# Fourier branch over even and odd parts, scans by halves of the groups, compressed scores of both heads at once, in a two-block float32 model

## The reference

```python
s = jnp.einsum('bgrcd,bgnd->bgrcn', qc, kc) * ATTN_SCALE          # compressed scores, 31 keys
p_cmp = masked_softmax(s, cmp_end[None, :] <= tpos[:, None])
o_cmp = jnp.einsum('bgrcn,bgnd->bgrcd', p_cmp, vc)

def _fourier_mix(u):                                              # u: 512 tokens x 512 channels
    ug = u.reshape(b, l, FOURIER_GROUPS, FOURIER_GROUP_CH)        # 4 groups of 128 channels
    f = jnp.fft.fft2(ug, axes=(1, 3), norm='ortho').real
    return f.reshape(b, l, FOURIER_WIDTH)

def _ssm_direction(ug, ..., reverse):                             # 32 groups, 64 complex states
    bu = jnp.einsum('blgc,gnc->blgn', ug, b_bar)
    _, h = lax.associative_scan(_scan_combine, (a, bu), axis=1, reverse=reverse)
    return jnp.einsum('blgn,gcn->blgc', h, c_mat).real            # forward and backward are added

merged = gates[..., :D_MODEL] * (y_f @ w_fourier_out) + gates[..., D_MODEL:] * (y_s @ w_ssm_out)
x = x + merged @ w_out
x = x + _hier_moe(hn, ...)                                        # 64 experts, 1024 -> 512 -> 1024
```

## Time and profile before

| | us |
|---|---|
| time, median of 3 runs | 2460.68 |
| lowest and highest of them | 2452.25, 2461.19 |
| the profiled execution | 2447.28 |
| its span, first to last instruction | 2445.4 |
| TensorE busy | 2226.5 (91%) |
| VectorE busy | 612.2 (25%) |
| ScalarE busy | 323.1 (13%) |
| GpSimd busy | 206.8 (8%) |
| mean granted TensorE clock | 0.971 of full |

### The profile page before, as it was taken

The page is one execution under the profiler, slowest core; times in us unless marked ns, Lnnn a source line. Parts: engine busy times, 40 slices in busy tenths (PEclk is TensorE's granted clock), DMA queues, the critical chain, the costliest instruction groups (busy, mean ns, idle before and its releaser), DMA issues.

```text
span 2445.4 us, 20383 instructions
## 1 busy us (share of the span) xinstructions
PE 2226.5 (91%) x8284; PEld 1022.6 (42%) x8284; DVE 612.2 (25%) x1311; ACT 323.1 (13%) x652; POOL 206.8 (8%) x186
## 2 busy tenths in 40 slices
PE   8999999999999999999999999988888888877886
PEld 4554444445444444466644463333323333322332
DVE  2246544311633210033431142111111111111114
ACT  2014424202111100021110120000000000000001
POOL 0001111010344200000000001000000000000001
PEclk9999999999999999998999999998999999999998
DMA  6201010322232321219422339999999999999995
GB/s 273 86 35 69 35 69 4 151 103 78 95 118 79 141 77 72 101 52 161 155 102 83 159 156 408 426 426 426 425 426 426 426 427 427 425 425 422 421 426 221
DMA packets 69759, 552.43 MB, mean 226 GB/s; under 512 B 21656, under 2 KB 26392, under 8 KB 37600
## 3 DMA queue, kind: packets, MB, share of 16 engines
q1 hardware_dynamic: 42384, 515.49, 51.8%
q10 hardware_dynamic: 17200, 23.23, 3.2%
q0 software_dynamic: 10080, 12.38, 1.4%
HBM read 543.91 MB, written 35.68 MB: 237 GB/s over the span
## 4 chain that ended last, share of the span: by engine, by line
PE 69%; DMA 26%; DVE 3%; ACT 1%; issue 1%; DVEq 0%; POOL 0%; SPq 0%; ACTq 0%; POOLq 0%
PE ps L380 25%; DMA sb<-in_eu 12%; PE ps L1008 9%; PE ps L456 8%; DMA sb<-in_eg 8%; PE ps L698 8%; PE ps L1040 4%; DMA sb<-in_ed 4%; PE ps L399 2%; PE ps L856 2%; PE ps L628 2%; PE ps L541 1%; PE ps L574 1%; PE ps L568 1%; DMA sb<-in_mgg 1%
## 5 line engine op out<-in xcount | busy, mean ns | idle before, releaser
L380 PE MATMUL ps<-sb 128*128 128x512 f32 (+2 forms) x1536 | 613.8, 559 | 2.8 <-issue 1.4
L1008 PE MATMUL ps<-sb 128*64 128x512 f32 x2048 | 487.7, 632 | 108.6 <-DMA sb<-in_eu 79.3
L380 PEld LDWEIGHTS ps<-sb 128*128 128x128 f32 x1536 | 279.7, 190 | 315.9 <-issue 312.6
L1008 PEld LDWEIGHTS ps<-sb 128*64 128x64 f32 x2048 | 176.7, 145 | 398.8 <-issue 398.7
L1040 PE MATMUL ps<-sb 128*64 128x512 f32 x992 | 232.5, 623 | 26.9 <-ACT sb L1427 17.2
L456 PE MATMUL ps<-sb 128*128 128x512 f32 x512 | 236.1, 600 | 0.3 <-DMA sb<-in_mgg 0.3
L698 PE MATMUL ps<-sb 128*128 128x512 f32 x448 | 192.5, 592 | 0.7 <-ACT sb L1247 0.7
L1451 DVE TENSOR_TENSOR sb<-sb 128x32 f32<-128x32 f32 (+10 forms) x292 | 115.4, 412 | 115.7 <-PE ps L662 66.2
L1040 PEld LDWEIGHTS ps<-sb 128*64 128x64 f32 x992 | 73.7, 143 | 164.2 <-issue 137.6
L456 PEld LDWEIGHTS ps<-sb 128*128 128x128 f32 x512 | 91.3, 190 | 100.0 <-issue 98.9
L698 PEld LDWEIGHTS ps<-sb 128*128 128x128 f32 x448 | 85.0, 190 | 107.6 <-issue 107.6
(11 more groups left out here) (283 smaller groups left out, 1481.5 us busy)
## 6 DMA issues: line engine op xcount, KB each, us to landing
sb<-in_eg SPq DMA_DIRECT2D x64, 2048.0 KB, 33.6
sb<-in_eu SPq DMA_DIRECT2D x63, 2048.0 KB, 33.9
sb<-in_ed SPq DMA_DIRECT2D x63, 2048.0 KB, 32.4
sb<-in_m SPq DMA_DIRECT2D x16, 2048.0 KB, 7.4
sb<-in_mg SPq DMA_DIRECT2D x8, 1536.0 KB, 6.9
sb<-in_winF SPq DMA_DIRECT2D x5, 2048.0 KB, 7.3
sb<-in_mgg SPq DMA_DIRECT2D x4, 2048.0 KB, 8.0
sb<-in_wo SPq DMA_DIRECT2D x4, 2048.0 KB, 7.3
```

What stands on the lines that cost most here:

```text
L380: ins = pe.matmul(out, lhsT, rhs, start=k == 0, stop=k == len(pieces) - 1)
L1008: ins = pe.matmul(o[64 * e:64 * e + 64, :], x[:, k, 64 * e:64 * e + 64], weight(2 * mat + e)[:, 512 * k:512 * k + 512], start=k == 0, stop ...
```

## The change

Three things are changed.

1. **Fourier branch.** The transform over 512 tokens is folded. GpSimd makes the sum and the difference of token t and token 512-t (`EO[0]` and `EO[1]`, two instructions of 4x255 values a partition, the second operand read backwards, and two small ones for token 0). The channel transform is then cosine on the sums and sine on the differences, over 256 tokens: 16 products of 128 columns in 4 tiles, and 4 products of 128 columns with a single row for token 256 (`v256`), which ScalarE writes into row 0 of the odd part. The token transform takes 4 products of 512 columns for each channel group where it took 8. The table `dft` is half as large. TensorE waits for the semaphore `eo` where it waited for the copies of `ufT`. The products `within` stand in pairs before `yf` 2 and `yf` 3.
2. **Scans.** VectorE does the state space work in two halves of 16 groups. The first half starts after six of the eight backward copies and the `v` tiles of its groups; the last two copies come after its first six instructions. `borders(0)` still waits for `sp` at 4, which is now the first half; `borders(2)` waits for 8. The expert loads' first wait is `sp` at 8. GpSimd clears the border columns of `Sp` by halves, behind its new work.
3. **Compressed scores.** A turn covers both head halves of a token block: 8 products of 31 columns, three recurrent steps, 8 transposes, one more step. VectorE's steps after the mask addition cover 8x31 values and are 4 turns in place of 8.

```diff
-                for h in range(2):
-                    dve.wait_ge(*T.full("cs", i, h))
-                    if n > 3:
-                        dve.wait_ge(*T.full("ct", (n - 4) // 2, h))
+                    after(own(dve.tensor_reduce(st, s3, op=ALU.max, axis=AX.X)))
+                    dve.tensor_tensor(s3, s3, bc(st, 2, 31), ALU.subtract).then_inc(S("csub"), 1)
+                    yield 2
+                    dve.wait_ge(S("cexp"), i + 1)
...
+                    dve.tensor_tensor(s3, s3, bc(st, 2, 31), ALU.mult).then_inc(S("cprob"), 1)
+                    yield 1
+                    copy(("ct", i, 1), PCT[32:63, :, 128 * i:128 * i + 128],
+                         T.ap("ct", i, 1)[0:31, :].rearrange("p (a b) -> p a b", a=4))
+                    yield 1
```

```diff
-            for i in range(4):
-                for gp in range(2):
-                    o = open_tile(pe, ("vf", i, gp), any_bank())
-                    for q in range(2):
-                        ins = pe.matmul(o[:, 256 * q:256 * q + 256], ufT[:, 2 * gp + q, 128 * i:128 * i + 128], ck("cs"), start=True, stop=True)
-                    ins.then_inc(T.f("vf", i, gp), 1)
+            pe.wait_ge(S("eo"), 4)
+            for b in range(2):
+                for part in range(2):
+                    o = open_tile(pe, ("vf", b, part), any_bank())
+                    for g in range(4):
+                        ins = pe.matmul(o[:, 128 * g:128 * g + 128], EO[part][:, g, 128 * b:128 * b + 128],
+                                        ck("cs")[:, 128 * part:128 * part + 128], start=True, stop=True)
+                    ins.then_inc(T.f("vf", b, part), 1)
...
-                chain(o, [(Vf[:, k % 4, g, 128 * (k // 4):128 * (k // 4) + 128], cf[:, k // 4, k % 4, :]) for k in range(8)], ("yf", g))
+                chain(o, [(Vf[part][b][:, g, :], cf[:, part, b, :]) for b in range(2) for part in range(2)], ("yf", g))
...
             gate_tile(0, 0, 0)
+            pe.wait_ge(S("sp"), 8)
             borders(2)
```

```diff
-            pool.wait_ge(S("sp_in"), 1)
-            pool.memset(Sp[0:64, :, :, 0], 0.0).then_inc(S("sp_zero"), 1)
-            pool.memset(Sp[64:128, :, :, 63], 0.0).then_inc(S("sp_zero"), 1)
+            for m in range(4, 8):
+                pool.wait_ge(*T.free("z2", m))
+            pool.wait_ge(S("m2w"), 7)
+            for n, op in enumerate((ALU.add, ALU.subtract)):
+                pool.tensor_tensor(EO[n][:, :, 1:256], ufT[:, :, 1:256], ufT[:, :, 511:256:-1], op).then_inc(S("eo"), 1)
+            pool.tensor_copy(EO[0][:, :, 0:1], ufT[:, :, 0:1]).then_inc(S("eo"), 1)
+            pool.memset(EO[1][:, :, 0:1], 0.0).then_inc(S("eo"), 1)
```

More of the change, by code:

```diff
@@ L288, in program @@
         Sp = view(zone, 16384, 2, 32, 64)
-        Vf = view(WR[2], 0, 4, 4, 256)
+        EO = [view(WR[2], 1024 * n, 4, 256) for n in range(2)]
+        Vf = [[view(WR[2], 2048 + 1024 * part + 512 * b, 4, 128) for b in range(2)] for part in range(2)]
         YS = view(zone, 4096, 32, 64)
@@ L1360, in scalar_program @@
             act.wait_ge(S("m2w"), 7)
-            for i in range(4):
-                for gp in range(2):
-                    copy(("vf", i, gp), Vf[:, i, 2 * gp:2 * gp + 2, :], T.ap("vf", i, gp).rearrange("p (a b) -> p a b", a=2))
+            for b in range(2):
+                for part in range(2):
+                    copy(("vf", b, part), Vf[part][b], T.ap("vf", b, part).rearrange("p (a b) -> p a b", a=4))
+                if b == 0:
+                    act.wait_ge(*T.free("vf", 0, 1))
+                    copy(("v256",), Vf[1][0][0:1], T.ap("v256")[0:1, :].rearrange("p (a b) -> p a b", a=4))
             for g in range(4):
@@ L1626, in cmp_scores @@
                                           bc(ck("cneg")[:, 31 * i:31 * i + 31], 1, 4), ALU.add).then_inc(T.s("cs", i, h), 1)
+                    for h in range(2):
                         dve.wait_ge(*T.free("cs", i, h))
-                        after(own(dve.tensor_reduce(st, s3, op=ALU.max, axis=AX.X)))
-                        dve.tensor_tensor(s3, s3, bc(st, 2, 31), ALU.subtract).then_inc(S("csub"), 1)
-                        dve.wait_ge(S("cexp"), n + 1)
-                        after(tt(s3, s3, bc(ck("c01")[:, 31 * i:31 * i + 31], 1, 4), ALU.mult))
@@ new lines, in cmp_scores @@
+                    after(tt(s3, s3, bc(ck("c01")[:, 31 * i:31 * i + 31], 1, 8), ALU.mult))
+                    after(own(dve.tensor_reduce(st, s3, op=ALU.add, axis=AX.X)))
+                    after(ts(st, st, 1e-20, None, ALU.max))
+                    after(own(dve.reciprocal(st, st)))
+                    if i == 0:
+                        dve.wait_ge(S("gate"), 1)
+                    after(tt(st, st, gate[:, i, :].rearrange("p (hd c) -> p hd c", c=3)[:, :, 0], ALU.mult))
+                    dve.tensor_tensor(s3, s3, bc(st, 2, 31), ALU.mult).then_inc(S("cprob"), 1)
@@ L1935, in fl @@
+            for g8 in range(4):
+                back(0, g8)
+            for g8 in range(2):
+                back(1, g8)
+            dve.wait_ge(S("ep"), 1)
             def fl(a):
                 return a.rearrange("p a b -> p (a b)")
-            own(dve.tensor_tensor_scan(fl(ar), fl(RHO), fl(vr), 0.0, ALU.mult, ALU.add))
-            after(own(dve.tensor_tensor_scan(fl(ai), fl(RHO), fl(vi), 0.0, ALU.mult, ALU.add)))
-            tt(vr, ar, er, ALU.mult)
-            after(tt(vi, ai, ei, ALU.mult))
@@ L2284, in gpsimd_program @@
             pool.memset(Ep[:, 1, :, 0], 0.0).then_inc(S("ep_one"), 1)
-            pool.wait_ge(S("sp_in"), 1)
-            pool.memset(Sp[0:64, :, :, 0], 0.0).then_inc(S("sp_zero"), 1)
-            pool.memset(Sp[64:128, :, :, 63], 0.0).then_inc(S("sp_zero"), 1)
+            for m in range(4, 8):
[5 more added lines that the diff above has]
+            pool.memset(EO[1][:, :, 0:1], 0.0).then_inc(S("eo"), 1)
+            for hf in range(2):
+                gs = slice(16 * hf, 16 * hf + 16)
+                if hf == 0:
+                    pool.wait_ge(S("eo"), 4)
+                else:
+                    pool.wait_ge(S("sp_zero"), 2)
+                pool.wait_ge(S("sp_in"), hf + 1)
+                pool.memset(Sp[0:64, :, gs, 0], 0.0).then_inc(S("sp_zero"), 1)
+                pool.memset(Sp[64:128, :, gs, 63], 0.0).then_inc(S("sp_zero"), 1)
             pool.wait_ge(S("mg2"), 8)
@@ L2402, in sync_program @@
                 fours("z2", g, 8)
-            load(("dft", 0), A["dft"])
+            load(("dft", 0), A["dft"], 2048)
             load(("mbr", 0), mbr_d.rearrange("p a b -> p (a b)"))
@@ L2703, in host @@
     a5 = 2 * np.pi * (np.outer(n, n) % 512) / 512
-    o["dft"] = np.concatenate([rows(np.cos(a5)), rows(-np.sin(a5))], 1).astype(np.float32)
+    odd = -np.sin(a5[:256])
+    odd[0] = np.cos(np.pi * n)
+    o["dft"] = np.concatenate([rows(np.cos(a5[:256])), rows(odd)], 1).astype(np.float32)
     o["eg"], o["eu"], o["ed"] = (g["expert_w_%s_2" % n][0] for n in ("gate", "up", "down"))
```

144 lines of the change are left out of this document (72 added, 72 removed).

## The result

The changed kernel takes 2423.28 us, the median of 4 runs (2422.39 to 2433.82). Runs of the kernel before on the same chip gave 2456.47 us (4 runs, 2449.67 to 2461.19). The ratio is 0.9887, 95% interval 0.9864 to 0.9911: faster by 1.1%. The profiled execution took 2433.82 us, with a span of 2432.0.

What follows compares the result with a forecast made beforehand. TensorE was taken to bound the kernel until the experts' loads, whose stream then sets the pace. Gains of 16.1 us (Fourier branch) and 3.5 us (scores) sum to 19.6, from 2460.7 to 2441.1 us; range 2431 to 2453.

Steps and rivals of the forecast that it cites:

- Token transform, 13.9 us less: In the Fourier branch, four `yf` tiles with half the products take 3.47 us less each, 13.9 us in all.
- Channel transform, 10.3 to 8.1 us: Fourier branch's 40 records of 128 columns, partly at low clock: 2.2 us less; bounds 4.3 less (6.0 us), 0.7 more.
- The rival of a low clock that lasts into the first `yf` tile: Low clock through the channel transform and into `yf` costs 4.6 us: gain 15.0, 2445.7 us; chance 0.13.
- The stage, 45 to 29 us: From the first channel product to `borders(0)`: about 29 us, was 45, with no wait ahead of the channel products.
- GpSimd at nothing: GpSimd's sums and differences, 1.9 to 3.1 us each, are hidden under the `v` products and cost nothing.
- Scans by halves: VectorE's state work in halves: `sp` 4 at about 1161 us, `sp` 8 at about 1182, both before TensorE asks.
- Part 2 removes a wait of 13 us that part 1 would open: At `borders(0)`, unhalved scans would hold TensorE until 1186 us; halving them prevents this, with no gain of its own.
- Compressed scores, 3.5 us less: TensorE's waits in the scores stage fall from 5.6 to 2.1 us: 3.5 us less, bounds 0 and 5.6.
- Products and steps are the same in number: Premise for the compressed scores: TensorE's work there is unchanged in number, so only its 5.6 us of waits counted.
- The end moves by the same amount: TensorE's gain before 1442 us moves the experts' load stream's start and the kernel's end equally; rival "gain lost": 0.10.
- The base: The starting time the summed gain of 19.6 us was taken from: the median of the runs, 2460.7 us.
- and I take the same amount from it: Final sum: 19.6 us taken from the runs' median, 13.4 us above the profiled execution, giving 2441.1 us.

Runs made afterwards that it cites:

- e4: The whole change run again beside its three parts on the same chip, against the kernel before: 2428.83 us (6 runs), ratio 0.9907.
- part 1 alone: The Fourier edits only, with scans and scores as before, against the kernel before: 2455.07 us (12 runs), ratio 1.0021.
- e10: The changed kernel with the third channel chain moved ahead of the first `within` and the wait for `z`, nothing added: 2424.62 us (5 runs), ratio 0.9893.
- e11: The changed kernel with the third channel chain ahead of the wait for `z`, plus added products before `z2` and `v`'s second half: 2417.98 us, ratio 0.9870.

## Why the prediction was right and wrong

- *Token transform, 13.9 us less:* right. A tile takes 3.49 us.
- *Channel transform, 10.3 to 8.1 us:* 7.4 us. The low clock ended a little sooner, and in an execution that keeps the clock (e4) it takes 5.9, the bound named for it. The rival of a low clock that lasts into the first `yf` tile didn't come.
- *The stage, 45 to 29 us:* 28.4 in the profile. Behind it 0.6 us more: the prediction let TensorE wait for `mg2` 0 as before, and it didn't.
- *GpSimd at nothing:* right; 2.69 us each inside bounds of 1.9 to 3.1, and one run with fourfold sums showed the cover.
- *Scans by halves:* 1024 values took 1.18 us and a scan 2.28, as worked out between 512 and 2048. `v` starts 2.25 us later in this execution; less that, `sp` 4 came at 1161.9 and `sp` 8 at 1183.3 us, against 1161 and 1182. "Part 2 removes a wait of 13 us that part 1 would open": 13.53 us. What the step missed is the price of that wait. It isn't 13 us of idling alone: the clock falls and takes 9 us more. So part 1 alone was a loss of 5 us, where the prediction's numbers leave it a small gain.
- *Compressed scores, 3.5 us less:* the waits went from 5.6 to 2.8 us with another 0.8 us in fewer groups of transposes (8 x 0.53 against 4 x 0.87), about as forecast (the terms of a turn on VectorE add up to 3.7 us, not the 4.1 given, and the trace has 3.9, 153.73 to 157.62). The step that failed is "Products and steps are the same in number". The number is the same, but the time isn't: the products went from 8 x 1.00 to 4 x 1.01 us, as the two heads' records ran side by side. This term of the sum was mis-sized by 4 us, 7.6 for 3.5, and lay above its own upper bound of 5.6, which was set by the waits alone.
- *The end moves by the same amount:* right. From the experts' loads to the end it took 1003 to 1005 us in every profile of the changed versions, though they were issued anywhere from 1413 to 1428 us.
- *The base:* the stages give 24.3 us where the sum had 19.6, so 5 of the 18 us. The larger part is what the sum was taken from. The three runs shown had a median of 2460.7 us; 63 later ones have 2451.4, and the profiled execution, at 2447.3, was nearer to that. From 2451.4 the sum of 19.6 would have given 2431.8 and the stages' 24.3 give 2427.1; the ten runs of the changed kernel have a median of 2428.2. The 17.8 us between forecast and result are thus 4.7 from the stages, 9.3 from the base (2460.7 for 2451.4) and 3.8 by the luck of the first four runs of the changed kernel, which came out at 2423.3. The step that failed is "and I take the same amount from it": with three runs that spread over 9 us, the profile's own 2447 should have had weight, and the range should have reached below 2431 for it.

What stays open is why executions of one kernel differ by 10 to 20 us. The profiles narrow down where. From the experts' loads to the end all fourteen took 1002.9 to 1005.3 us, though behind 1420 us the granted clock was at its low level for 106 to 156 us in sum, so what sets these executions apart lies ahead of the loads. The two profiled executions of the changed kernel (2433.82 and 2428.12 us) are 5.7 us apart, and as much at the issue of those loads (1427.55 and 1421.88). The slower one lost 6.6 us of clock at one place in the first block:

```profile
107.97 12.71 PE L381 MATMUL ps<-sb 128*128 128x62 f32 x64 [1.38 <-issue]
```

With the same gap of 1.38 or 1.39 us these records took 7.33 us in twelve of the fourteen profiles. The other one in which they took longer, 12.77 us, is that of e10, with 2433.25 us the slowest of its five runs. Over the 63 runs of before, the time falls with the mean clock (correlation -0.63), which leaves more than half of the variance to something else. No run was made on what decides whether the clock falls at such a gap.

## What to carry to other kernels

Before taking products out ahead of a wait, ask what that wait then does to TensorE's clock: the work behind it gets dearer, so cover and shortening belong together, and where real work can stand in the gap, put it there. Where small products use half of the rows, issue those of the two halves in turn, so that they run side by side. And take a forecast from all that is known of the base, not from three runs.

## What the runs showed of the hardware

- A gap of about a microsecond can cost the clock, and its length alone doesn't decide. Ahead of `v`'s second half the gap was 0.62 to 1.19 us in eleven profiles and the 64 records took 11.7 to 12.8 us in ten of them, 7.36 in one (e4, a gap of 0.67); in the three with the gap filled to 0.2 us or less they took 7.25 to 7.36. But a gap of 0.62 us ahead of `borders(2)` in e11, behind 512-column products, left 7.36 us, and one of 1.38 us ahead of 64 records of 62 columns cost the clock in two of fourteen profiles. Gaps of 0.95 us between 128-column and 512-column products, ahead of the first `yf` tile, left the clock at 1.00.
- 31-column products over 64 rows: records in one half of the rows start 0.11 us apart, and records in the other half run beside them, 0.007 us behind, at no further cost. From the last to the next 128-row product it is 0.20 us.
- 128-column records: 2.00 us for 16 at full clock, 0.125 each, also where one row of the output is all that is wanted (1.03 us for 8).
- GpSimd's sum with one operand read backwards took 2.69 us for 1020 values, beside 1.94 us for 1024 and 1.53 for 512 in the earlier trace rows, so 0.75 us more than the forward one of the same size. In the fourfold run the same instruction took between 2.3 and 3.2 us. Whether the backward read is the reason was not tested.
